# A routed mixture-of-experts layer whose experts are taken in falling order of their block counts, by a table that VectorE makes

## The reference

```python
logits = (ht @ w_router).astype(jnp.float32) + b_router.astype(jnp.float32)
top_val, top_idx = lax.top_k(logits, TOP_K)          # T = 256 tokens, TOP_K = 4, N_EXPERTS = 32
gates = jax.nn.softmax(top_val, axis=-1)
...
def expert_block(args):
    xblk, e = args
    gu = xblk @ w_gate_up[e] + b_gate_up[e]           # 1024 x 2048
    gate = jnp.minimum(gu[:, :D_EXPERT], SWIGLU_LIMIT)
    up = jnp.clip(gu[:, D_EXPERT:], -SWIGLU_LIMIT, SWIGLU_LIMIT)
    act = gate * jax.nn.sigmoid(SWIGLU_ALPHA * gate) * (up + 1)
    return act @ w_down[e] + b_down[e]                # 1024 x 1024
...
out = jax.ops.segment_sum(y, buf_tok, num_segments=T + 1)[:T]
```

## Time and profile before

| | us |
|---|---|
| median of 3 runs | 1252.61 |
| lowest, highest | 1247.39, 1253.58 |
| the profiled execution | 1249.92 |
| its span, first to last instruction | 1248.2 |
| first item's gate-and-up begins | 303.09 |
| items in all | 51 |

### The profile page before, as it was taken

The page is one execution under the profiler, slowest core; times in us unless marked ns, Lnnn a source line. Parts: engine busy times, 40 slices in busy tenths (PEclk is TensorE's granted clock), DMA queues, the critical chain, the costliest instruction groups (busy, mean ns, idle before and its releaser), DMA issues.

```text
span 1248.2 us, 28051 instructions
## 1 busy us (share of the span) xinstructions
PE 1055.7 (85%) x11069; PEld 524.6 (42%) x11070; DVE 309.1 (25%) x862; ACT 185.3 (15%) x403; POOL 109.3 (9%) x217
## 2 busy tenths in 40 slices
PE   3999999999996666668999999976669699969996
PEld 1777876645442222223444444432224244424443
DVE  0266445445221111111222222211112122212223
ACT  2331124424110000001111111100001011101112
POOL 7020002030100000000000000000000001000000
PEclk9899999998997887887999999997789799989998
DMA  9942136898999999999999969999999999999665
GB/s 367 408 166 90 68 137 226 335 387 297 428 426 427 426 427 429 425 427 429 428 427 428 426 276 427 423 427 428 428 427 425 428 428 429 425 428 428 258 272 216
DMA packets 49521, 455.85 MB, mean 365 GB/s; under 512 B 4790, under 2 KB 5916, under 8 KB 17104
## 3 DMA queue, kind: packets, MB, share of 16 engines
q1 hardware_dynamic: 43152, 417.91, 80.6%
q10 hardware_dynamic: 4960, 33.09, 6.4%
q0 software_dynamic: 1376, 4.38, 1.1%
HBM read 454.29 MB, written 1.07 MB: 365 GB/s over the span
## 4 chain that ended last, share of the span: by engine, by line
PE 54%; DMA 17%; SPq 15%; DVE 8%; issue 2%; another core or an unknown queue 1%; ACT 1%; ACTq 0%; DVEq 0%
PE bank L2017 21%; DMA raw<-in_w_gate_up 11%; PE bank L2031 10%; SPq L409 8%; PE bank L1582 7%; SPq L421 4%; DMA dn<-in_w_down 4%; PE bank L1989 3%; SPq L425 3%; PE bank L1908 2%; PE bank L2040 2%; DVE aT L1478 1%; DMA raw<-in_w_in 1%; DVE gated L1463 1%
## 5 line engine op out<-in xcount | busy, mean ns | idle before, releaser
L2017 PE MATMUL bank<-raw,xT 128*32 128x512 f32 x1600 | 214.6, 683 | 89.8 <-DMA raw<-in_w_gate_up 82.4
L2017 PE MATMUL bank<-odd,xT 128*32 128x512 f32 x1664 | 206.1, 644 | 48.0 <-DMA odd<-in_w_gate_up 48.0
L1463 DVE TENSOR_TENSOR gated<-bank,bias_i 128x256 f32<-128x256 f32 x51 | 21.6, 424 | 612.9 <-PE bank L2040 612.9
L2017 PEld LDWEIGHTS bank<-raw,xT 128*32 128x32 f32 x1600 | 55.6, 119 | 232.3 <-issue 132.0
L938 ACT ACTIVATE evg<-bank 128x512 f32<-128x512 f32 x51 | 30.5, 597 | 708.8 <-PE bank L2017 708.8
L2017 PEld LDWEIGHTS bank<-odd,xT 128*32 128x32 f32 x1664 | 57.9, 115 | 180.3 <-issue 117.2
L661 POOL TENSOR_TENSOR gatehot<-onehot,gates 128x128 f32<-128x128 f32 x102 | 54.9, 557 | 896.8 <-PE bank L2005 859.8
L2031 PE MATMUL bank<-raw,aT 128*32 128x256 f32 x2016 | 118.7, 380 | 7.7 <-DVE aT L1478 7.5
L1582 PE MATMUL bank<-hT,raw 128*128 128x256 f32 (+1 forms) x496 | 113.8, 388 | 2.2 <-DMA raw<-in_w_in 2.2
L1582 PEld LDWEIGHTS bank<-hT,raw 128*128 128x128 f32 (+1 forms) x496 | 93.2, 190 | 19.8 <-issue 3.0
L2031 PEld LDWEIGHTS bank<-raw,aT 128*32 128x32 f32 x2016 | 64.4, 110 | 55.2 <-issue 17.1
(11 more groups left out here) (411 smaller groups left out, 834.7 us busy)
## 6 DMA issues: line engine op xcount, KB each, us to landing
raw<-in_w_gate_up SPq DMA_DIRECT2D x64, 2048.0 KB, 33.8
odd<-in_w_gate_up SPq DMA_DIRECT2D x61, 2048.0 KB, 44.3
dn<-in_w_down SPq DMA_DIRECT2D x16, 2048.0 KB, 42.8
raw<-in_w_down ACTq DMA_DIRECT2D x31, 1024.0 KB, 11.4
raw<-in_w_down SPq DMA_DIRECT2D x15, 2048.0 KB, 39.4
raw<-in_w_down SPq DMA_DIRECT2D x19, 1024.0 KB, 39.1
dn<-in_w_down SPq DMA_DIRECT2D x16, 1024.0 KB, 42.1
raw<-in_w_in SPq DMA_DIRECT2D x7, 2048.0 KB, 17.0
```

What stands on the lines that cost most here:

```text
L1463: body.step("gate", tt(gated[:, :, :, :], turned[:, :, 0:2, :], bias_i[:, :, 0:2].unsqueeze(3).to_broadcast([P, 4, 2, CAP]), ALU.add))
L2017: g = mm(bank[5][j * CAP:(j + 1) * CAP, :], xT[:, u % 2, u // 2, :], gu_slab(u, p)[:, j * NC:(j + 1) * NC], start=u == 0, stop=u == KT - 1)
```

## The change

VectorE sorts the experts by falling `nblk` (ties: the higher number first). The experts 0, 1 and 2 keep the first three places, since two of them are already loaded and the third is asked for before the sort is done. The sort is made by comparisons: a 32 x 32 table `versus` of keys for the rank, a second one of places that is multiplied with `nblk` and summed for the first item of each expert, then the list of items and the list of experts by place (`order`), each turned from a column into a row by a 32 x 32 transposition. `first_item` and `last_item` are now indexed by the place and not by the expert. SP and ACT read from `order` the expert whose weights a transfer brings; the engines that loop over items wait for all seven tables (`TABLES`) where they waited for four. The small matmul of PE that turned the item list is gone.

```diff
@@ the sync engine @@
-            sp.wait_ge(S("items_ready"), 3)
+            sp.wait_ge(S("items_ready"), 2)
...
-                    load_gu(sp, e + 1, v, p)
+                    load_gu(sp, e, v, p)
+
+            def expert_at(n):
+
+                return sp.value_load(order[0:1, n], min_val=0, max_val=NE - 1)
...
-            next_gu(1, before, 0)
+            next_gu(2, before, 0)
+            sp.wait_ge(S("items_ready"), TABLES)
             with sp.Fori(1, NE // 2 - 1) as q:
                 for p in range(2):
...
-                    next_dn(e, before, p)
+                    next_dn(expert_at(bass.ds(n, 1)), before, p)
@@ GpSimd @@
-            pool.wait_ge(S("items_ready"), 4)
+            pool.wait_ge(S("items_ready"), TABLES)
@@ ScalarE @@
             def last_slab(e, after):
 
+                act_e.wait_ge(S("items_ready"), TABLES)
+                following = act_e.value_load(order[0:1, e], min_val=0, max_val=NE - 1)
                 act_e.wait_ge(S("dn_mm"), 4 * after)
-                load_dn(act_e, e + 1, 3, 0)
+                load_dn(act_e, following, 3, 0)
@@ VectorE, ahead of take_xT(0) @@
-            step(v.tensor_tensor_scan(ends[:, 1:NE + 1], ones[:, 0:NE], nblk[:, :], 0.0, ALU.mult, ALU.add))
...
+            step(v.tensor_tensor_scan(ends[:, 1:4], ones[:, 0:3], nblk[:, 0:3], 0.0, ALU.mult, ALU.add))
+            v.tensor_copy(first_item[:, 0:4], ends[0:1, 0:4]).then_inc(S("items_ready"), 1)
+            ts(last_item[:, 0:3], ends[0:1, 1:4], -1.0, None, ALU.add).then_inc(S("items_ready"), 1)
+            v.tensor_copy(spans[:, 0, :], slots[:, :])
+            step(stt(key[:, :], nblk[:, :], float(NE), slots[:, :], ALU.mult, ALU.add))
+            step(ts(key[:, 0:3], slots[:, 0:3], -1.0, -float(NE * NE), ALU.mult, ALU.add))
@@ VectorE, behind take_xT(0) @@
+            step(tt(versus[:, :, :], key[:, :].unsqueeze(1).to_broadcast([P, NE, NE]),
+                    key[:, :].unsqueeze(2).to_broadcast([P, NE, NE]), ALU.is_gt))
+            step(v.tensor_reduce(rank[:, :], versus[:, :, :], AX.X, ALU.add))
+            step(ts(seat[:, :], rank[:, :], -1.0, None, ALU.add))
+            step(ts(seat[:, 0:3], slots[:, 0:3], -5.0, None, ALU.add))
+            step(tt(versus[:, :, :], seat[:, :].unsqueeze(1).to_broadcast([P, NE, NE]),
+                    seat[:, :].unsqueeze(2).to_broadcast([P, NE, NE]), ALU.is_lt))
+            step(tt(versus[:, :, :], versus[:, :, :], nblk[:, :].unsqueeze(1).to_broadcast([P, NE, NE]), ALU.mult))
+            step(v.tensor_reduce(rank[:, :], versus[:, :, :], AX.X, ALU.add))
...
+            v.tensor_copy(order[:, :], until[0:1, 0, :]).then_inc(S("items_ready"), 1)
+            v.tensor_copy(last_item[:, 3:NE], until[0:1, 1, 3:NE]).then_inc(S("items_ready"), 1)
+            ts(n_items[:, :], until[0:1, 1, NE - 1:NE].to_broadcast([1, 2]), float(1 - NE), None, ALU.add).then_inc(S("items_ready"), 1)
+            ts(first_item[:, 4:NE + 1], until[0:1, 1, 3:NE], 1.0, None, ALU.add).then_inc(S("items_ready"), 1)
@@ TensorE @@
-            pe.wait_ge(S("sel_ready"), 3)
-            mm(bank[2][0:1, 3 * P:4 * P], isum[:, 0:1], ident[:, :], start=True, stop=True).then_inc(S("rank_mm"), 1)
```

More of the change, by code:

```diff
@@ L45 @@
 MAXB = T // CAP
+TABLES = 7
 KSTEPS = 4
@@ L140, in build @@
         gate2q = moe("gate2q", [P, NQ])
+        sort = Region(base + 18 * SLOT + 2048)
+        key = sort("key", [P, NE])
+        rank = sort("rank", [P, NE])
+        seat = sort("seat", [P, NE])
+        spans = sort("spans", [P, 2, NE])
+        hits = sort("hits", [P, 3, NE])
+        sort = Region(base + 17 * SLOT)
+        versus = place("versus", [P, NE, NE], BF16, sort.at)[0]
+        until = sort("until", [P, 3, NE])
+        column = sort("column", [P, 3, NE])
+        row = sort("row", [P, 3, NE])
         assert moe.at <= base + 19 * SLOT
@@ L149, in build @@
         ones = moe("ones", [P, P])
+        order = place("order", [1, NE], I32, moe.at)[0]
         hsum = moe("hsum", [P, CAP])
@@ L650, in _ @@
             keep(stri[:, :], [[1, P]], -1, -1)
-            g.iota(iota_p[:, :], pattern=[[0, 1]], base=-1, channel_multiplier=1,
-                   allow_small_or_imprecise_dtypes=True).then_inc(S("consts"), 1)
+            for q in range(CT):
+                rows = slice(q * CAP, (q + 1) * CAP)
+                step(g.iota(item_of[rows, :], pattern=[[CAP, 3]], base=-1, channel_multiplier=1,
+                            allow_small_or_imprecise_dtypes=True))
+                step(g.iota(seat_of[rows, :], pattern=[[0, 1]], base=-4, channel_multiplier=1,
+                            allow_small_or_imprecise_dtypes=True))
+            g.memset(found[:, :], 0.0).then_inc(S("consts"), 1)
             def weigh(i):
@@ L986, in _ @@
                         item(i)
-                    last_slab(e, after)
+                    last_slab(bass.ds(e + 1, 1), after)
             after = act_e.value_load(first_item[0:1, NE - 2:NE - 1], min_val=1, max_val=NI)
@@ L994, in _ @@
                 if p == 0:
-                    last_slab(NE - 2, after)
+                    last_slab(slice(NE - 1, NE), after)
             a.activation(spare[:, :], ident[:, 0:1], ACT.Sqrt)
@@ L1406, in _ @@
             take_xT(0)
[L1407 to L1410, removed]
-            step(stt(pos[:, :, :], pos[:, :, :], 1.0, sel[:, :, :], ALU.add, ALU.mult))
@@ new lines, in _ @@
+            step(tt(versus[:, :, :], seat[:, :].unsqueeze(1).to_broadcast([P, NE, NE]),
+                    seat[:, :].unsqueeze(2).to_broadcast([P, NE, NE]), ALU.is_lt))
+            step(tt(versus[:, :, :], versus[:, :, :], nblk[:, :].unsqueeze(1).to_broadcast([P, NE, NE]), ALU.mult))
+            step(v.tensor_reduce(rank[:, :], versus[:, :, :], AX.X, ALU.add))
+            tt(spans[:, 1, :], rank[:, :], nblk[:, :], ALU.add)
+            step(stt(pos[:, :, :], rank[:, :].unsqueeze(1).to_broadcast([P, TT, NE]), float(CAP), ranks, ALU.mult, ALU.add))
@@ new lines, in _ @@
+            tt(hits[:, :, :], item_of[:, :].unsqueeze(2).to_broadcast([P, 3, NE]),
+               rank[:, :].unsqueeze(1).to_broadcast([P, 3, NE]), ALU.is_ge)
+            step(tt(until[:, :, :], item_of[:, :].unsqueeze(2).to_broadcast([P, 3, NE]),
+                    spans[:, 1:2, :].to_broadcast([P, 3, NE]), ALU.is_lt))
+            step(tt(hits[:, :, :], hits[:, :, :], until[:, :, :], ALU.mult))
+            tt(until[:, :, :], hits[:, :, :], slots[:, :].unsqueeze(1).to_broadcast([P, 3, NE]), ALU.mult)
@@ new lines, in _ @@
+            step(stt(pos[:, :, :], pos[:, :, :], 1.0, sel[:, :, :], ALU.add, ALU.mult))
+            step(v.tensor_reduce(found[:, 0:3], until[:, :, :], AX.X, ALU.add))
+            step(ts(column[:, :, :], found[:, 0:3].unsqueeze(2).to_broadcast([P, 3, NE]), -1.0, 0.0, ALU.add, ALU.max))
+            step(v.transpose(row[:, :, :].rearrange("p c e -> p (c e)"), column[:, :, :].rearrange("p c e -> p (c e)")))
+            v.tensor_copy(items[:, :], row[0:1, :, :].rearrange("p c e -> p (c e)")[:, 0:NI + 3]).then_inc(S("items_ready"), 1)
@@ new lines, in _ @@
+            step(ts(key[:, :], seat[:, :], seat_of[:, 0:1], None, ALU.is_equal))
+            step(tt(hits[:, 0:2, :], spans[:, :, :], key[:, :].unsqueeze(1).to_broadcast([P, 2, NE]), ALU.mult))
+            step(v.tensor_reduce(found[:, 3:5], hits[:, 0:2, :], AX.X, ALU.add))
+            step(ts(column[:, 0:2, :], found[:, 3:5].unsqueeze(2).to_broadcast([P, 2, NE]), -1.0, None, ALU.add))
+            step(v.transpose(until[:, 0:2, :].rearrange("p c e -> p (c e)"), column[:, 0:2, :].rearrange("p c e -> p (c e)")))
```

33 lines of the change are left out of this document (15 added, 18 removed).

## The result

The changed kernel takes 1291.22 us (median of 3 runs, 1290.26 to 1295.52), against 1252.61 before: a ratio of 1.034, 95% interval 1.0306 to 1.0373. The medians differ by 38.6 us, and the ratio stands for 42 (38 to 47). The profiled execution took 1290.26 us and its span is 1288.3, so 40.1 more than the span before.

What follows compares the result with a forecast made beforehand. The expert stage was taken as bound by transfers, with PE bounding the first places. Summed along PE: place 3 at 369.2, 805.4 after place 14, place 18 at 865.5, last expert 1248.6, span 1288.2, plus 1.7: 1290 us, range 1275 to 1302.

Steps and rivals of the forecast that it cites:

- The start: Up to place 3: the sort lies on PE's path and adds 8 us, bounds 5 to 10.
- Places 3 to 14: Twelve experts, 30 items: PE never waits for weights and takes 436 us, from 369.2 to 805.4.
- The transition: From place 15 to 18, where PE goes from work to waiting for the feed: 59.2 us, place 18 at 864.6.
- The last stage: Places 18 to 31, all of one item at the feed's pace: 13 x 29.47 us, the last starting at 1248.6.
- The end: Behind the last item, 10.5 us of output; the span ends at 1288.2, 40 more than before.
- the check from the feed: Start of place 18 worked out from the feed's last stop, at 559.1: 865.8 against 864.6; 865.5 was taken.
- The stops: Places 3 to 6: the feed stops about 29 us, then 13 to 14.5 each, 71 in all against 35 before.
- That the three-item experts cost nothing: Rival: experts of two refill a feed reserve and win back the stops of places 4 to 6; 1248 us, chance 0.05.
- That the feed never stops: Rival: the weight stream runs on from 306 without a stop; about 1207 us, chance 0.03.
- The last slab: Rival, places 3 to 14: reading `order` delays the last slab beyond its 1.4 us margin; 1302 us, chance 0.06.
- That the order is what it says: Rival to this: the sort leaves the experts nearly where they were; 1260 us, chance 0.02.
- That the reads of `order` cost nothing: SP's 0.28 us read hides behind its lead or queue, ACT's moves a few hundredths; without cover 30 reads would be 9 us.

Runs made afterwards that it cites:

- threes first: Changed kernel with keys putting only the three experts of three items at places 3 to 5, others in numbered order: 1273.32 us, ratio 1.0196 to the kernel before.
- the alternating order: Changed kernel with its sort, but places alternating light and heavy experts behind the first three: 1244.43 us, ratio 0.9962 to the kernel before.
- the sort alone: Changed kernel with all its sort, tables and reads, but keys leaving the experts in numbered order: 1256.97 us, ratio 1.0056 to the kernel before.
- small transfers: From the third expert, a quarter of each gate-and-up pair and half the first down pair transferred: kernel before 1065.99 us, changed kernel 1072.85.
- rising: Changed kernel with the sort's keys negated, so heavy experts come last: 1316.2 us, ratio 1.055 to the kernel before.
- five first: Changed kernel with keys putting only the five-item expert at place 3, others in numbered order: 1253.64 us, ratio 1.0044 to the kernel before.
- the short sort: Rank found on columns after transposing the key: changed kernel's falling order 1284.23 us, ratio 1.0287 to the kernel before; with alternating places 1240.92, ratio 0.9924.

## Why the prediction was right

**The start** was forecast at 8 us and measured 9.1 (23.25 between the first two items against 14.17). The chain on VectorE came out as priced: the large steps 1.21 and 1.22, the tables at 313.1 for 312.9, the wait of PE 6.41 for 6.6. Short was the price of the low clock behind it: 1.4 was allowed, about 2.7 came. From the gather's start to the start of `down` PE took 6.2 us in place of 3.8, and the granted clock was 0.50 over all of it (316.8 to 322.8). The sum over 1024 elements went at 1.22 and not at the price of the strided sum, so the upper bound of that term wasn't needed. The table row that the prediction cites (the Trainium skill, "VectorE: DVE Perf Modes", section on the TRN2 errata) would have had the large steps at 1.13 and the chain 3 us shorter, mostly by its 22 small steps at 0.1, where the trace has 0.21; the trace decides against it. The same section says below its table that this row comes out too low, and gives 151 cycles more than the elements for an fp32 `tensor_tensor` at 0.96 GHz. That is an estimate of 1.22 us for 1024, and the trace agrees (1.21 and 1.22).

**Places 3 to 14**: 436 forecast, 436.0 measured, with no wait for weights and the clock at 1.00. **The transition**: 59.2 forecast from place 15 to 18, 59.5 measured. **The last stage**: 13 x 29.47 forecast, 13 x 29.45 measured; the last expert at 1248.79 for 1248.6. **The end**: span 1288.3 for 1288.2. The start's 1.1 too little was made up by the 0.9 that the check from the feed had added at place 18, so that part of the agreement is luck. So is the agreement of 1290 with the profiled execution's 1290.26 to a fraction of a us: the three executions spread over 5.

**The stops** were forecast at 29 and 13 to 14.5 each; the windows give 27, 15, 13 and 14. One stop was not in the list: 6 us between 316 and 370, when the late start delays the first requests. The forecast had 36 us more of stops beside a span 40 longer, and said nothing of the 4 between them. The time hardly rested on that list, since the sum went along PE. Its rule for a stop, that the next request comes too late wherever PE isn't behind the feed, was too coarse: in threes first and in the alternating order an expert of three items made no stop though PE waited for nothing, because two experts' transfers had been asked for by then.

**The rivals.** That the three-item experts cost nothing is refuted where they stand together (15, 13 and 14 us of stops; threes first, 17.5 us beyond the sort alone), and its grain of truth is measured by the alternating order, where they lose nothing. That the feed never stops is refuted by the hole at 0.15 (its own sum, 1190 and 15.8, gives 1206 and not 1207, which changes nothing). The last slab was never late: PE has no wait for weights from 370 to 806. That the order is what it says is seen in PE's names: the expert at place 3 has five items, from 370.51 to the one of 427.34. That the reads of `order` cost nothing that can be seen is shown twice: by the small transfers, where no wait for each expert comes with them, and by the last stage at full transfers, where an expert takes 29.45 us with them and 29.47 without. The chance for slower, 0.92, stood on the right mechanism.

## What to carry to other kernels

With two sets of buffers, the transfers for the step after next can be asked for only when the last part of a step begins. The feed stops when all that was asked for has landed by then. So two heavy steps in a row cost what their work is longer than their feed (here 44 less 29.5 for each further expert of three items), and with light steps between them the same steps cost nothing (the alternating order from 460 us on); a step as long as five items stopped the feed for about 26 us at the front and in the alternating order, and for 24 near the end. It is the spacing of the requests that counts. Put a light step between heavy ones, and leave no heavy step at the end, where nothing is left to transfer beside it. Before sorting anything at run time, look at whether the sort lies on the path at a place where nothing else is late, and do it on columns. And a window whose edge lies inside a hole of the feed makes two holes of one: before a stop is put down to an expert, find the request that ends it in SP's timeline.

## What the runs showed of the hardware

Nearly the same wait of PE costs different amounts behind it. In the seven executions with the long sort PE waited 5.96 to 6.66 us for the one-hot matrix. In four of them (rising 5.96, threes first 6.16, five first 6.19, the sort alone 6.29) the second item began 21.8 to 21.9 us behind the first, and in three (changed 6.41, alternating 6.54, small transfers 6.66) 23.3, where 14.2 is the undisturbed time. So the part beyond the wait is 1.4 to 1.7 us in the four and 2.5 to 2.7 in the three. With the short sort PE waited only 2.3 and 2.5 us, and 1.5 was lost beyond the wait all the same. The granted clock fell to 0.50 during the wait, and what differs is how long it stayed there: in the changed kernel until 6 us behind the gather's start, with the sort alone until about 3. Why it rose at different times isn't shown.

The first item of the expert stage begins between 301.2 and 307.6 us in the profiled executions of kernels whose first part is the same work, which is the size of the spread between runs; differences of a few us had to be read from a place to a place within one trace.
